# The convolution branch's input projections are computed in the scan instead of in the input stage

## The reference

```python
def short_conv_branch(pa, conv_w):
    u, gate_b, gate_c, z = jnp.split(pa, 4, axis=-1)
    cu = gate_c * u
    y = conv_w[0] * shift_prev(cu) + conv_w[1] * cu + conv_w[2] * shift_next(cu)
    return gate_b * y * jax.nn.silu(z)
```

## Time and profile before

| | us |
|---|---|
| median of 3 runs | 3682.78 |
| the profiled execution, time | 3688.47 |
| the profiled execution, span from first to last instruction | 3686.7 |
| PE busy in the span | 3296.3 (89%) |
| mean granted TensorE clock | 0.926 |

### The profile page before, as it was taken

One profiled execution on the slowest core, in us unless ns is written; L12 is line 12 of the kernel. 1 busy time (PEld: TensorE's weight loads), 2 busy tenths in 40 slices (PEclk: granted clock), 3 DMA queues, 4 the chain that ended last, 5 costly groups with the idle time before them and its releaser, 6 DMA issues. The chain is left out here.

```text
span 3686.7 us, 62343 instructions
## 1 busy us (share of the span) xinstructions
PE 3296.3 (89%) x27450; PEld 2755.4 (75%) x27450; DVE 1805.7 (49%) x2463; ACT 1178.6 (32%) x1648; POOL 393.9 (11%) x272
## 2 busy tenths in 40 slices
PE   5599999798986689897999989998777999999999
PEld 3488888688886479855899977776546788888887
DVE  6454455455653542253555534753443463636364
ACT  0444334222222322255444422542552211111111
POOL 0122221000000112110000012211102000000000
PEclk9799999778876899999999999999788999999999
DMA  8112231422212321324112013122002111111112
GB/s 346 43 70 101 105 125 72 122 72 72 72 43 94 131 92 46 117 85 173 57 59 63 31 61 126 47 78 94 29 18 86 52 40 57 42 56 43 54 45 76
DMA packets 145995, 294.53 MB, mean 80 GB/s; under 512 B 10048, under 2 KB 86976, under 8 KB 140224
## 3 DMA queue, kind: packets, MB, share of 16 engines
q1 hardware_dynamic: 126608, 212.95, 17.1%
q0 software_dynamic: 19120, 77.60, 6.2%
HBM read 211.22 MB, written 79.30 MB: 79 GB/s over the span
## 5 line engine op out<-in xcount | busy, mean ns | idle before, releaser
L60 PE MATMUL ev_ps<-h_hi,ev_w_hi 128*128 128x512 f32 (+1 forms) x792 | 288.5, 364 | 36.5 <-POOL ev_w_lo L360 35.2
L60 PE MATMUL ff_ps<-h_hi,ff_w_hi 128*128 128x512 f32 x768 | 300.1, 391 | 2.2 <-DVE ff_w_lo L3043 2.2
L61 PE MATMUL ff_ps<-h_lo,ff_w_hi 128*128 128x512 f32 x768 | 299.8, 390 | 0.0
L62 PE MATMUL ff_ps<-h_hi,ff_w_lo 128*128 128x512 f32 x768 | 299.7, 390 | 0.0
L62 PE MATMUL ev_ps<-h_hi,ev_w_lo 128*128 128x512 f32 (+1 forms) x792 | 281.1, 355 | 0.0
L61 PE MATMUL ev_ps<-h_lo,ev_w_hi 128*128 128x512 f32 (+1 forms) x792 | 281.1, 355 | 0.0
L3043 DVE TENSOR_TENSOR ff_w_lo<-ff_w,ff_w_hi 128x1024 fp32r<-128x1024 f32 (+1 forms) x80 | 89.5, 1119 | 339.5 <-ACT ff_w_hi L3018 339.5
L60 PEld LDWEIGHTS ev_ps<-h_hi,ev_w_hi 128*128 128x128 f32 x792 | 150.5, 190 | 75.1 <-POOL ev_w_lo L360 36.0
L3018 ACT ACTIVATE ff_w_hi<-ff_w 128x1024 fp32r<-128x1024 f32 (+1 forms) x80 | 78.0, 975 | 326.3 <-PE ff_ps L62 324.0
L60 PEld LDWEIGHTS ff_ps<-h_hi,ff_w_hi 128*128 128x128 f32 x768 | 144.8, 189 | 34.0 <-DVE ff_w_lo L3043 3.8
L62 PEld LDWEIGHTS ff_ps<-h_hi,ff_w_lo 128*128 128x128 f32 x768 | 144.8, 189 | 30.3
(11 more groups left out here) (501 smaller groups left out, 8065.7 us busy)
## 6 DMA issues: line engine op xcount, KB each, us to landing
ff_w<-in_w_up SPq DMA_DIRECT2D x48, 512.0 KB, 3.5
ev_w<-in_ev_w_in POOLq DMA_DIRECT2D x33, 512.0 KB, 3.9
...
sc_ar<-ar SPq DMA_DIRECT2D x20, 512.0 KB, 6.1
```

Of the source, the lines that this page charges most:

```text
L60: nc.tensor.matmul(out, w_hi, x_hi, start=start, stop=False)
L61: nc.tensor.matmul(out, w_hi, x_lo, start=False, stop=False)
L62: return nc.tensor.matmul(out, w_lo, x_hi, start=False, stop=stop)
```

## The change

The 16 tiles u, gc, gb and z leave the input stage, which now runs 17 tiles: the low-rank one, then k, r, v, zb for each p. Its matmul groups, ACT's list and DVE's list are reordered: the low-rank products of the first direction follow the r groups instead of the k groups, those of the second follow the v groups (two of the three together after the last) instead of the gc groups, zb comes at the end of its slice, the bonus after the next slice's k tile. `sw` and `ic` get one buffer for each direction, `kd` loses one. The split input h (high and low, `h_even`) is stored to DRAM.

The scan takes the 16 tiles over as 80 units: five token chunks of 256, each with 16 weight tiles, 24 matmuls of 258 columns a unit (256 tokens and a neighbour on either side). Eight units run in a body: 0 after the first state_w, 1 before the transposes, 2 after them, 3 to 7 between the levels. They get the two banks bA, so `gram`, transposes, level_p and level_z now all share the two banks bB, and `gram` runs as four turns of half the size, each waiting until DVE has masked the one before. The weights are loaded and split again for each chunk, with two raw tiles. ACT copies u and applies silu to z, DVE makes the convolution and the gates (`convolve`). To make room in SBUF, ar goes from three buffers to two, bk, v and y from two to one, and so SP loads chunk n + 1 in body n, after the store of y of chunk n - 1.

The diff, cut to its core:

```diff
-    KIND = ["lora", "zb"] + [x for p in range(4) for x in ["k", "r", "v", "u", "gc", "gb", "z"] + (["zb"] if p < 3 else [])]
+    KIND = ["lora"] + [x for p in range(4) for x in ("k", "r", "v", "zb")]
...
-                    sp.wait_ge(gated, p + 1)
-                    sp.dma_start(g.mixT[p], res[:]).then_inc(mix_st, 16)
+                        if d == 0:
+                            sp.wait_ge(mixed, 2 * (shift_no(at["v", p]) + 1))
+                            sp.dma_start(g.vT[:, p], mv[:]).then_inc(v_st, 16)
+                            store_zb(p)
+                            if p < 2:
+                                sp.dma_start(g.hT[p], h[p][:].bitcast(F32)).then_inc(h_st, 16)
                     sp.wait_ge(bon_out, NG * (p + 1))
                     sp.dma_start(g.bonT[p], t1[:]).then_inc(bon_st, 16)
...
-                        if kind == "gc":
-                            lora_products(i, 1, b)
-                        if kind == "zb" and i and b == 0:
-                            bonus(i - 1, 0)
-                            bonus(i - 1, 1)
-                        if kind == "zb" and i and b == 1:
-                            bonus(i - 1, 2)
+                        if kind == "v" and b >= 1:
+                            lora_products(i, 1, b - 1)
+                        if kind == "v" and b == 2:
+                            lora_products(i, 1, 2)
+                        if kind == "k" and i and b == 2:
+                            for c in range(NG):
+                                bonus(i - 1, c)
...
-        St, tmp, y = sb("S", [P, 2, 4, CH]), sb("Stmp", [P, 2, 4, CH]), sb("y", [P, 2, 2, 4, P])
+        St, tmp, y = sb("S", [P, 2, 4, CH]), sb("Stmp", [P, 2, 4, CH]), sb("y", [P, 2, 4, P])
...
+        w, w_hi, w_lo = sb("w", [P, 2, KD, P]), sb("w_hi", [P, 2, KD, P], F32R), sb("w_lo", [P, 2, KD, P], F32R)
+        hs, h_hi, h_lo = sb("h_stage", [P, 2, KD, HW]), sb("h_hi", [P, KD, HW], F32R), sb("h_lo", [P, KD, HW], F32R)
+        ub, cu, yb, sz, res = sb("u", [P, HW]), sb("cu", [P, HW]), sb("conv", [P, TOK]), sb("silu", [P, TOK]), sb("gated", [P, 2, TOK])
...
+                        if n >= 2:
+                            done(sp, "YS", d, n - 2)
+                        sp.dma_start(ar[:, n % 2, d].rearrange("c p k t -> c (p k) t"),
...
+                        if n:
+                            done(sp, "trBK", d, n - 1)
+                        sp.dma_start(bk[:, d].rearrange("c p k t -> c (p k) t"),
...
+                        sp.dma_start(vt[:, d], g.vT[:, :, at:at + P]).then_inc(ld[d, n % 2], 16)
...
+                def load_h(c):
+                    if c:
+                        sp.wait_ge(conv["h_hi"], c)
+                        sp.wait_ge(conv["h_lo"], c)
+                    a, z = max(TOK * c - 1, 0), min(TOK * c + TOK + 1, T)
+                    for x in range(2):
+                        sp.dma_start(hs[:, x, :, a - TOK * c + 1:z - TOK * c + 1], g.hT[x][:, :, a:z]).then_inc(h_loaded, 16)
+
+                def store_conv(j):
+                    c, p = j // 4, j % 4
+                    sp.wait_ge(conv["out"], j + 1)
+                    sp.dma_start(g.mixT[p][:, TOK * c:TOK * c + TOK], res[:, j % 2]).then_inc(res_stored[j % 2], 16)
...
+                    if n + 1 < NB:
+                        load(n + 1)
+                    if n % 2 == 0 and n // 2 + 1 < T // TOK:
+                        load_h(n // 2 + 1)
+                    if n < NB:
+                        store_conv(2 * n)
+                        store_conv(2 * n + 1)
...
-                def gram(n, x):
+                def gram(n, x, turn):
...
+                        elif x == 0:
+                            done(pe, "mB", d, n, 0)
+                        elif turn == 0:
+                            done(pe, "mB", d, n, 1)
                         else:
-                            done(pe, "mB", d, n)
...
+                    settle()
+                    for p in range(4):
+                        for q in range(2):
+                            for d in range(2):
+                                r, c = half((turn + d) % 2), half(q)
+                                last = mm(bB[d][c, 128 * p:128 * p + 128], bk[r, d, p, x, c], ar[r, n % 2, d, p, :, c], start=True, stop=True)
+                                if p == 3 and q == 1:
+                                    last.then_inc(S[("gB", "gK")[x], d], 1)
...
+                def project(n, k):
+                    x = SLOTS * n + k
+                    c, p, kind = UNITS[x]
+                    pe.wait_ge(conv["w_lo"], x + 1)
+                    if x % PER == 0:
+                        pe.wait_ge(conv["h_hi"], c + 1)
+                        pe.wait_ge(conv["h_lo"], c + 1)
+                    if x >= 2:
+                        cb, pb, before = UNITS[x - 2]
+                        pe.wait_ge(conv[{"u": "u", "gc": "cu", "gb": "gb", "z": "z"}[before]], 4 * cb + pb + 1)
+                    for k in range(KD):
+                        last = product(nc, bA[x % 2][:, 0:HW], (w_hi[:, x % 2, k], w_lo[:, x % 2, k]), (h_hi[:, k], h_lo[:, k]), k == 0, k == KD - 1)
+                    last.then_inc(conv["done"], 1)
...
-                        gram(n, 0)
+                        gram(n, 0, 0)
                     if old:
                         state_w(n - 1, 0)
                     if new:
-                        gram(n, 1)
+                        project(n, 0)
+                        gram(n, 0, 1)
+                        gram(n, 1, 0)
                     if old:
                         state_u(n - 1, 0)
                     if new:
+                        gram(n, 1, 1)
+                        project(n, 1)
                         turn_v(n)
-                        turn_bk(n, 0)
                     if old:
                         state_ys(n - 1, 0)
                     if new:
+                        turn_bk(n, 0)
                         turn_bk(n, 1)
+                        project(n, 2)
                         mask_v(n)
                         level_p(n, 0)
                     if old:
                         state_w(n - 1, 1)
                     if new:
                         level_z(n, 0)
+                        project(n, 3)
                         level_p(n, 1)
                     if old:
                         state_u(n - 1, 1)
                     if new:
                         level_z(n, 1)
+                        project(n, 4)
                         level_p(n, 2)
                     if old:
                         state_ys(n - 1, 1)
                     if new:
                         level_z(n, 2)
+                        project(n, 5)
                         level_p(n, 3)
                         level_z(n, 3)
+                        project(n, 6)
                         last_p(n)
+                        project(n, 7)
                         last_z(n)
...
+                def low_part(x):
+                    pool.wait_ge(conv["w_hi"], x + 1)
+                    if x >= 2:
+                        pool.wait_ge(conv["done"], x - 1)
+                    nc.gpsimd.tensor_tensor(w_lo[:, x % 2], w[:, x % 2], w_hi[:, x % 2].bitcast(F32), ALU.subtract).then_inc(conv["w_lo"], 1)
...
+                    for x in range(SLOTS * n + 2, min(SLOTS * n + SLOTS + 2, NU)):
+                        low_part(x)
+                        if x + 2 < NU:
+                            weight(x + 2)
...
+                def convolve(n, k):
+                    x = SLOTS * n + k
+                    c, p, kind = UNITS[x]
+                    j, bank = 4 * c + p, bA[x % 2]
+                    if kind == "gc":
+                        dve.wait_ge(conv["done"], x + 1)
+                        dve.wait_ge(conv["u"], j + 1)
+                        tt(cu[:], bank[:, 0:HW], ub[:], ALU.mult).then_inc(conv["cu"], 1)
...
+                        wc = [col(g, "conv_w", 4 * tap + p) for tap in range(3)]
+                        nc.vector.tensor_scalar(yb[:], cu[:, 0:TOK], wc[0], None, ALU.mult).then_inc(conv["taps"], 1)
+                        for tap in (1, 2):
+                            dve.wait_ge(conv["taps"], 3 * j + tap)
+                            stt(out=yb[:], in0=cu[:, tap:tap + TOK], scalar=wc[tap], in1=yb[:], op0=ALU.mult, op1=ALU.add).then_inc(conv["taps"], 1)
+                    if kind == "gb":
+                        dve.wait_ge(conv["done"], x + 1)
...
+                        tt(res[:, j % 2], bank[:, 1:TOK + 1], yb[:], ALU.mult).then_inc(conv["gb"], 1)
+                    if kind == "z":
+                        dve.wait_ge(conv["z"], j + 1)
+                        dve.wait_ge(conv["gb"], j + 1)
+                        tt(res[:, j % 2], res[:, j % 2], sz[:], ALU.mult).then_inc(conv["out"], 1)
...
                         level_add(n, 2)
+                        convolve(n, 5)
                     if old:
                         output(n - 1, 1)
                     if new:
                         level_mask(n, 3)
...
```

(17 more changed lines are left out.)

291 lines of the change are left out of this document (151 added, 140 removed).

## The result

The changed kernel takes 3761.81 us, the median of 4 runs (3752.93 to 3767.86), against 3682.78 us (3677.57 to 3697.24): a ratio of 1.0206, with a 95% interval of 1.0168 to 1.0245. It is 2% slower. The profiled execution took 3767.47 us (span 3765.5), so 79 us more than the profiled one of before.

What follows compares the result with a forecast made beforehand. PE was taken to bound both the input stage and the scan. 3688.5 (profiled) - 174 (input stage) + 253 (scan) = 3767, its median 5.7 lower, 3762; leaned down to a forecast of 3755 us, range 3705 to 3815.

Steps and rivals of the forecast that it cites:

- the first body: Scan's first body: eight units cost 23 us, a wait for h about 8, a few won back by clock; +28 us.
- Input stage: Input stage with 17 tiles: 75 us a slice, 174 us gained in all, between 150 and 195.
- the ring of DVE and ACT: Input stage: the chain through DVE and ACT ends a slice at 72 to 77 us, against 66.6 by PE alone.
- Units: Scan bodies: eight projection units of 2.9 us each at full clock add 23.2 us a body.
- gram in four turns: Scan bodies: masks and latency between gram's turns on one pair of banks make PE wait, +1.75 us a body.
- The taps before level 3: Scan bodies: DVE work including three taps delays the mask between levels 3 and 4; +3 us a body.
- The clock: Scan bodies: units between the levels raise PE's clock from 0.81 to full, -8.2 us a body.
- Rival 3: Scan: the clock does not rise, a third of the units run at half; 90 us a body, total 3915; chance 0.10.
- The loads: Scan bodies: the next gram waits for loads issued after y's store; +4.5 us a body, bounds 0 and 8.
- Rival 1: Scan absorbs its units, loads in time, POOL misses taps: body 65, input stage -195, total 3669; chance 0.13.

Runs made afterwards that it cites:

- e3: Changed kernel with the second direction's low-rank products moved to zb's groups and the first direction's exponentials before the second's sigmoids; 3763.9 us.
- e7: Changed kernel with a slice's bonus products moved behind the first group of the next slice's r tile, first-direction low-rank products one group later; 3763.4 us.
- e10: e9 with the second direction's last low-rank products and sigmoids later and its key scale before zb's silu; 3693.5 us.
- e2: Changed kernel with POOL computing the scan weights' low parts for one of eight blocks only; 3752.4 us.
- e6: e1 with bk and v loaded in mid-body, ar before y's store, and the split h behind everything else; 3703.2 us.
- e8: e6 with only two of a unit's eight blocks multiplied, 6 matmuls of 24; 3658.4 us.
- e1: Changed kernel with unit 5's three taps on DVE moved behind level 3's addition; 3747.8 us.
- e9: e6 with unit 0 after gram's second turn, small tables ahead of the first loads, and only h's first column cleared; 3703.6 us.
- e12: e10 with all six loads of a chunk (ar, bk, v) together, just before y's store; 3682.5 us.

## Why the prediction was right, and where it was not

**The total.** 3755 forecast, 3762 measured; slower, by the forecast's path. The parts were less right than their sum. Before it was leaned down to 3755 the sum stood at 3762, the measured time, and that is luck: the first body was 10.5 us longer than forecast, the other nine some 6 us shorter together, and the input stage gave 4 us more.

**Input stage: right.** Forecast 75 us a slice and -174; measured 74.3, 74.3, 72.8 between the kk products, and -177.9 (runs with the same input stage differ by up to 5 us in where the scan begins). PE waits at the bonus as forecast (3.4 us a slice). That the ring of DVE and ACT sets the slice was half of it: e3 and e7 moved its links without shortening it, e10 shortened it by 1.7 us.

**Units: right.** 2.9 us each, 23.0 a body at full clock.

**gram in four turns: right.** 1.7 and 0.72 us between turns, 2.4 in all against before's 1, so +1.4 where the forecast had +1.75.

**The taps before level 3: right in place and size.** Forecast +3, measured 3.56 in every body, 1.9 of it POOL's (e2). It had another price that the term left out: the clock falls behind it, 3.5 us.

**The clock: right in direction, half the size.** Forecast -8.2 by full clock; measured 0.93, about 9.8 us of a body at half clock instead of 18.2, so -4.2. e6 shows that the two waits were what kept it from full (0.99 without them, in bodies 2 to 7). That the wide matmuls raised it fits e8, 0.79 with a quarter of them, but e8's longer stalls are a rival that no run took away. Rival 3, at 90 us a body, is refuted.

**The loads: the step that failed.** Forecast +4.5 a body; measured 4.9 us in four of eight bodies, 0.6 a body. The batch took its 15 us, but PE's work after y took 14.4 us in the body shown, not the 11.9 that I added up at full clock: level_z 3 and unit 6 at half clock, 3.5 us longer together, filled the time in which the load was late. The term for the taps and the term for the loads were added as if independent. They lay beside each other: while one wait stood, the other cost nothing, and with the first taken away the second showed in full (e1: 6.1 us a body, more than the 4.5). The half clock missed by one term and the wait missed by the other cancelled, 4.0 against 3.9. That they should is in part this coupling; that they did so to a tenth is luck.

**The first body: mis-sized.** Forecast +28, measured +38.5. Its window has clock 0.79, where I had counted on a gain; PE waits 8.1 us for h as forecast, and some of what followed ran at half clock (units 0, 3 and 6 took 5.1, 7.1 and 5.1 us). With the taps moved (e1) it is +29, and in e9, with its other orders at the scan's start, +25, though a wait of 7.7 us is left there, now ahead of a turn of gram.

**Rival 1, the faster side, was refuted, but its mechanism exists.** It wanted bodies of 65 by a batch in time and taps not in the way. e12 has just these, body 65.2, and ends at even, not at 3669. In its trace the first gram starts at 490.4, so the stage, with e10's order, gained 183 where the rival had 195, and 17.2 x 9 + 24 are 179.
